# One hybrid decoder layer on eight cores: shared q/k/v weight pieces for two tiles, GLA steps in the next stage, stores from the scrap buffer

## The chip, the cores and the metric

The kernel runs on all 8 cores of one Trainium2 chip. Each core computes the whole layer for one of the 8 batch entries (4096 rows of 1024), and no core talks to another. The metric is the device time in microseconds of the slowest core. The kernel before takes 1694.6 us (median of 3 runs, 1691.15 to 1695.91).

## The reference

For x of one batch entry (4096 x 1024) the layer computes, in short:

```python
h = rms_norm(x, g_pre)
qa, ka, va, za, qb, kb, vb, zb, lr, gate_a, gate_b = split(h @ w_in)   # 5648 columns
# mixer A: 4 heads, two q/k maps of 64 each, causal, ALiBi
p = softmax(q k^T / 8 + bias);  oa = (p[0] - lam * p[1]) @ v
ya = (rms_norm(oa, g_sub_a) * (1 - lam_init) * silu(za)) @ w_up_a
# mixer B: gated linear attention, 4 heads, key 64, value 128
glog = log_sigmoid(lr @ w_alpha + b_alpha) / 16      # lr: 16 columns of the projection
S_t = diag(exp(glog_t)) S_{t-1} + k_t^T v_t ;  ob_t = q_t S_t
yb = (rms_norm(ob, g_sub_b) * silu(zb)) @ w_up_b
y = sigmoid(gate_a) * ya + sigmoid(gate_b) * yb
out = x + rms_norm(y @ w_out, g_post)
```

## The kernel before, in words

The 4096 rows are cut into 8 tiles of 512. After a prologue there is one stage per tile, t = 0 to 7, and a tail. In stage t the attention of tile t (4 heads, 4t+4 blocks of 128 keys each, two blocks per step) is the base load; between its steps TensorE is given "units" of the other work, taken from one list in order. `stage_units(t)` makes the list, each unit has a cost, and `pump` takes units so that their cost keeps pace with the attention steps. The list of stage t is, in order:

- head of E: the first four merge-gate chains of tile t-1 (`GA0`, `GB0`), and `za` of tile t (SiLU gate of mixer A);
- the rest of E(t-1): gates and the two up-projections; then F(t-1): the output projection, the post-norm and the residual (`u_f`), whose `fin(s)` adds x and stores 128 rows;
- gproj(t): low-rank decay (`wlr`, `walpha`), `vb`, `zb`, q/k of mixer B; merged into it, from stage 1 on, `a_units(t+1)`: load x, norm, and transposes of the next tile into `hT`;
- `u_qkv(t+1)`: q, k and v of mixer A for the next tile, with the GLA steps of tile t (`g_khat`, then per 128 rows `g_at`, `g_o`, `g_s`, `g_ew`, `g_tr`, `g_ew2`) merged into it. The last stage has no `u_qkv`, and there the GLA steps follow gproj.

A "chain" is 8 matmuls of 512 columns into one PSUM bank. Five banks rotate among all units and the attention scores. All engines run their instructions in the order of the program text, and a wait at the head of one holds everything behind it.

Weights come in "pieces" (1 MB of float32). The first time, a piece is loaded in four DMAs of 256 KB to a staging area (8 buffers, two pieces), converted to bf16 by VectorE and ScalarE in turn, and written back to DRAM (`wsc`, 512 KB); later it is loaded from there. The converted pieces live in a ring of 7 slots (`wring`), filled in the order of `wseq`: `emit_load` issues the next load, `acquire` takes a piece, `release` frees it. The q/k/v pieces are six: `QA0, QA1, KA0, KA1, VA0, VA1`. All input DMAs stand in SyncE's queue, in order. The stores (`out`, `wsc`) stand in GpSimd's.

x arrives in three buffers `xb0..2` (and four more in the prologue): for the residual of F and for the norm of the next tile. In `fin(s)` VectorE writes the result over the x buffer, GpSimd stores that buffer, and the next x load into it (`x_load(sem)`) waits for the store. The scrap buffer `scr` has six parts, `s0..s5`: F uses s0 to s3 (two per 128 rows, in turn), the E gates too, the decay `gl` (s0, s1), `cum` (s2, s3) and `eb` (s4, s5), and the GLA output o of a step stands in `gl`, that is s0 or s1. The low-rank projection is 8 matmuls that write 16 PSUM partitions each.

`posts` are the pieces of work at the end of each attention head (norm, gate, transpose of the head's output); `run_post` runs one.

## Time and profile before

| | |
|---|---|
| median of 3 runs | 1694.6 us (1691.15 to 1695.91) |
| the profiled execution, its own time | 1694.94 us |
| its span on the slowest core (core 4) | 1693.4 us; the cores lie between 1667.6 and 1693.4 |
| busy: TensorE, VectorE, ScalarE, GpSimd | 1449.6, 874.9, 850.1, 172.0 us |
| DMA, mean | 124 GB/s; 176.09 MB read from and 32.51 MB written to HBM |
| stage ends of 0, 1, 2, ... 7 (about) | 187, 383, 563, 753, 952, 1167, 1394, 1632 us |

TensorE is busy 86% of the span and is what all stages turn on; the other engines are half used. So the page is read by stretches: where TensorE stands still, what it waits for, and at which clock it runs. A "busy" matmul counts from its start to a modelled end, and neighbours overlap, so 100% busy is a full pipeline. "PEclk" is the granted clock as a share of 2.4 GHz; in single stretches it is 1.00 or 0.50.

### The profile page before, as it was taken

The page shows a single profiled execution, that of the slowest core. Times are in us where ns is not written, and L with a number is a line of the kernel's source. Part 1 is how long each engine was busy: PE and PEld are TensorE (multiplying, and loading weights), DVE is VectorE, ACT ScalarE, POOL GpSimd, SP SyncE. Part 2 cuts the span into 40 slices and gives each one's busy share as a digit, 9 for nine tenths or more (in the row PEclk, how much of TensorE's full clock was granted, in tenths as well). Part 3 has the DMA queues.
Part 4 walks back from the last instruction along what each step waited for, and adds up shares of the span by engine and source line. Part 5 has one row for each costly group of instructions (what it writes and reads, how often), then busy time and mean ns, then how long its engine had stood idle before and what let it go on. Part 6 is the DMA issues. An engine that isn't in the chain of part 4 may idle for free.

```text
span 1693.4 us, 28068 instructions; the slowest of 8 cores (1667.6 to 1693.4 us)
## 1 busy us (share of the span) xinstructions
PE 1449.6 (86%) x10512; PEld 756.4 (45%) x10512; DVE 874.9 (52%) x2292; ACT 850.1 (50%) x1714; POOL 172.0 (10%) x247
## 2 busy tenths in 40 slices
PE   3686769779987999889988999888997999998887
PEld 1233324344434454445544554445554555544443
DVE  2467646565546636563446544365335562342564
ACT  2451344514552456435573456735666656667532
POOL 1111101110010001110010000101001010000001
...
GB/s 259 302 214 110 104 278 207 214 51 116 100 200 96 96 104 170 140 52 100 75 201 110 63 100 76 187 87 76 76 63 202 98 63 64 76 75 137 51 75 100
DMA packets 77232, 210.41 MB, mean 124 GB/s; under 512 B 9120, under 2 KB 27824, under 8 KB 77104
## 3 DMA queue, kind: packets, MB, share of 16 engines
...
q0 software_dynamic: 8928, 32.51, 4.8%
...
q10 hardware_dynamic: 1936, 0.94, 0.2%
...
HBM read 176.09 MB, written 32.51 MB: 123 GB/s over the span
## 4 chain that ended last, share of the span: by engine, by line
PE 58%; DVE 20%; ACT 9%; DMA 7%; issue 3%; POOL 2%; SPq 0%; POOLq 0%; DVEq 0%; ACTq 0%
PE ps_q L270 27%; PE ps_f L270 19%; PE ps_oa L270 10%; ACT sb_PT L947 4%; DMA sb_KT<-w_in 3%; DMA sb_xb<-x 2%; DVE sb_gtB L745 2%; DVE sb_state L721 2%; DVE sb_ATs L731 2%; DMA out<-sb_xb 1%; DVE sb_gtA L1002 1%; DVE sb_tmpo L975 1%; DMA sb_KT<-w_up_b 1%; DVE sb_xb L834 1%; ACT sb_wring L378 1%
## 5 line engine op out<-in xcount | busy, mean ns | idle before, releaser
L947 ACT ACTIVATE sb_PT<-ps_q 128x512 bf16<-128x512 f32 (+3 forms) x698 | 371.0, 568 | 333.2 <-PE ps_q L270 183.6
L270 PE MATMUL ps_oa<-sb_V,sb_PT 128*128 128x129 bf16 x4224 | 346.0, 223 | 10.7 <-DVE sb_tmpo L975 3.3
L270 PEld LDWEIGHTS ps_oa<-sb_V,sb_PT 128*128 128x128 bf16 x4224 | 289.6, 99 | 139.1 <-issue 30.0
L947 ACT ACTIVATE sb_PT<-ps_f 128x512 bf16<-128x512 f32 (+3 forms) x454 | 251.9, 567 | 152.4 <-PE ps_q L270 96.5
L270 PE MATMUL ps_q<-sb_hT,sb_wring 128*128 128x512 bf16 x1032 | 263.6, 392 | 20.0 <-ACT sb_wring L378 10.3
L270 PE MATMUL ps_f<-sb_hT,sb_wring 128*128 128x512 bf16 x760 | 196.3, 394 | 6.8 <-ACT sb_hT L596 4.1
L270 PE MATMUL ps_q<-sb_QT,sb_KT 64*128 64x512 bf16 (+3 forms) x698 | 167.9, 369 | 19.9 <-DVE sb_vb L664 4.9
L270 PE MATMUL ps_q<-sb_wring,sb_hT 128*128 128x512 bf16 x528 | 140.2, 405 | 20.4 <-DVE sb_eblast L655 7.4
L270 PEld LDWEIGHTS ps_q<-sb_hT,sb_wring 128*128 128x128 bf16 x1032 | 94.7, 100 | 133.9 <-issue 51.2
L270 PE MATMUL ps_f<-sb_QT,sb_KT 64*128 64x512 bf16 (+3 forms) x454 | 137.5, 368 | 14.1 <-DVE sb_KT L603 4.3
L270 PE MATMUL ps_f<-sb_wring,sb_hT 128*128 128x512 bf16 x496 | 130.1, 396 | 7.5 <-DVE sb_szA L619 3.6
L270 PEld LDWEIGHTS ps_f<-sb_hT,sb_wring 128*128 128x128 bf16 x760 | 69.8, 100 | 90.8 <-issue 32.6
L270 PEld LDWEIGHTS ps_q<-sb_wring,sb_hT 128*128 128x128 bf16 x528 | 49.6, 103 | 84.4 <-issue 46.1
L270 PE MATMUL ps_q<-sb_wring,sb_yT 128*128 128x512 bf16 x320 | 78.1, 379 | 8.8 <-DVE sb_scr L853 4.6
L997 POOL TENSOR_TENSOR sb_rstda<-sb_rsa,sb_lams 128x4 f32<-128x4 f32 x32 | 32.5, 1015 | 454.1 <-DVE sb_rsa L995 451.1
L796 DVE SCALAR_TENSOR_TENSOR sb_scr<-sb_scr,ps_q 128x512 f32<-128x512 f32 x40 | 27.4, 684 | 93.9 <-PE ps_q L270 93.8
L772 ACT ACTIVATE sb_scr<-ps_q 128x512 f32<-128x512 f32 x72 | 43.3, 603 | 63.6 <-PE ps_q L270 63.4
L378 ACT ACTIVATE sb_wring<-sb_KT,sb_smalls 128x256 bf16<-128x256 f32 (+1 forms) x72 | 35.9, 547 | 75.9 <-DVE sb_wring L382 57.7
L270 PEld LDWEIGHTS ps_f<-sb_wring,sb_hT 128*128 128x128 bf16 x496 | 45.2, 101 | 63.3 <-issue 28.7
L772 ACT ACTIVATE sb_scr<-ps_f 128x512 f32<-128x512 f32 x56 | 33.9, 606 | 54.8 <-PE ps_f L270 54.7
L270 PEld LDWEIGHTS ps_q<-sb_QT,sb_KT 64*128 64x128 bf16 x698 | 36.4, 94 | 55.8 <-issue 36.6
L1002 DVE SCALAR_TENSOR_TENSOR sb_gtA<-sb_oaf,sb_rstda,sb_szA 128x128 bf16<-128x128 f32 x128 | 45.7, 357 | 27.8 <-POOL sb_rstda L997 25.0
...
## 6 DMA issues: line engine op xcount, KB each, us to landing
...
```

The costliest lines, as they stand in the source:

```text
L270: P.op("pe", lambda e: e.matmul(out=out_, lhsT=lhsT, rhs=rhs, start=start, stop=stop, **kw), reads=reads, writes=writes)
L378: act(lambda e: e.activation(out=dst_ap, in_=src_ap, func=AF.Copy, scale=sc), rd, [key])
L721: dve(lambda e, c=c, hh=hh, r=r: e.scalar_tensor_tensor(out=state[r, c, :], in0=state[r, c, :], scalar=eblast[r, c, s:s + 1], in1=BANK[b][ ...
L731: dve(lambda e, hd=hd, i=i: e.scalar_tensor_tensor(out=ATs[:, hd, :], in0=o[:, hd * 128:(hd + 1) * 128], scalar=1.0, in1=o[:, hd * 128:(hd ...
L745: dve(lambda e, hd=hd, i=i, sl=sl: e.scalar_tensor_tensor(out=gtB[:, hd, :], in0=o[:, sl], scalar=rstdb[:, i:i + 1], in1=szB[:, s, sl], op ...
L772: act(lambda e: e.activation(out=dst, in_=BANK[b][:, :], func=AF.Tanh, scale=0.5), [b], [key])
L796: dve(lambda e: e.scalar_tensor_tensor(out=ta[j], in0=ta[j], scalar=1.0, in1=BANK[b][:, :], op0=ALU.add, op1=ALU.mult), [b, f"s{j}"], [f"s ...
L834: dve(lambda e, hh=hh: e.scalar_tensor_tensor(out=ap[:, hh * 512:(hh + 1) * 512], in0=zg[hh], scalar=rstdz[:, g:g + 1], in1=ap[:, hh * 512 ...
L947: act(lambda e, pp=pp, m=m, c0=c0, b=b, cbias=cbias: e.activation(out=PT[pp][:, m, c0:512], in_=BANK[b][:, c0:512], func=AF.Exp, bias=cbia ...
L975: dve(lambda e: e.tensor_tensor(out=tmpo[:, i0:i0 + n, :], in0=src[:, :, 0:128], in1=rz[:, i0:i0 + n].unsqueeze(2).to_broadcast([128, n, 1 ...
L997: pool(lambda e: e.tensor_tensor(out=rstda[:, c4], in0=rsa[:, c4], in1=lams[:, 5:6].to_broadcast([128, 4]), op=ALU.pow), [f"rsa{h}", "nhal ...
L1002: dve(lambda e, a=a: e.scalar_tensor_tensor(out=gtA[gi][:, a, :], in0=oaf[:, a, :], scalar=rstda[:, h * 4 + a:h * 4 + a + 1], in1=szA[:, a ...
```

## The change

1. Prologue. Tiles 0 and 1 share the q/k/v pieces: q and k of tile 0, q and k of tile 1, then v of both are computed before stage 0, and `wseq` loses one round of the six pieces (`QKV` for tile 1). Stage 0 has no `u_qkv` any more.
2. GLA steps. `core_units` takes the GLA steps of tile t-1 into the head of stage t, between the half chains of the head gates and of `za`; `merge` now puts side units also into the middle of a chain. In the last stage the steps of tile 7 still follow gproj. The output o of a step stands in `eb` (s4, s5) instead of `gl` (s0, s1).
3. Stores. `fin` writes its result over `scr` and stores from there; the x buffer is free once VectorE has read it.
4. Decay input. `wlr` gets 32 columns per k-chunk (16 of them zero); chunk k goes to one of four groups of 32 PSUM partitions, and `walpha`, repeated four times over the partitions, sums the groups in its own matmul. Both arrive in one array of the host, `w_alr`.
5. Constants move behind the first two weight pieces on SyncE's queue, `gpost` behind the prologue's q and k, and the first x load stands first. `run_post` runs once after each unit with a cost.

```diff
-            def lr_one(b, k, st_, sp_):
-                mm(BANK[b][0:16, :], wlr[:, k, :], hT[t % 2][:, k, :], st_, sp_, ["wlr"] + hkeys(t), [b])
+                g, half = k % 4, k // 4
+                mm(BANK[b][32 * g:32 * g + 32, :], wlr[:, 2 * g + half, :], hT[t % 2][:, 2 * g + half, :], half == 0, half == 1,
+                   ["wlr"] + hkeys(t), [b])
...
-            u_lr = chain(8, lr_one, lr_ev)
+            u_lr = chain(8, lr_one, lr_ev, 0.08)
...
-        wseq = QKV + SEQ_Z + SEQ_G + (QKV if ntiles > 1 else [])
+        wseq = QKV + SEQ_Z + SEQ_G
...
-            dve(lambda e: e.tensor_copy(out=gl[s % 2], in_=BANK[b][:, :]), [b], [f"s{s % 2}"])
+            dve(lambda e: e.tensor_copy(out=eb[s % 2], in_=BANK[b][:, :]), [b], [f"s{4 + s % 2}"])
...
                 for hh in range(2):
-                    dve(lambda e, hh=hh: e.scalar_tensor_tensor(out=ap[:, hh * 512:(hh + 1) * 512], in0=zg[hh],
+                    dve(lambda e, hh=hh: e.scalar_tensor_tensor(out=zg[hh], in0=zg[hh], scalar=rstdz[:, g:g + 1],
...
-                P.op("pool", lambda e: e.dma_start(out=out[g * 128:(g + 1) * 128, :], in_=ap), reads=keys, dma="st" + sem[1:])
+                P.op("pool", lambda e: e.dma_start(out=out[g * 128:(g + 1) * 128, :],
+                                                   in_=scr[:, 2 * (s % 2):2 * (s % 2) + 2, :].rearrange("p a b -> p (a b)")),
+                     reads=[f"s{2 * (s % 2)}", f"s{2 * (s % 2) + 1}"], dma=f"st{s % 2}")
                 x_load(sem)
...
             for i, u in enumerate(main):
                 res.append(u)
-                if u[2]:
-                    continue
...
+        def core_units(k, gap):
+            none = (gap, lambda: None, False)
+            core = [w(0.6 * k, g_khat), none]
+            for s in range(4):
+                core += [w(0.3 * k, g_at, s)]
+                core += [z(g_ew2, s - 1)] if s >= 1 else [none]
+                core += [w(0.6 * k, g_o, s), w(0.3 * k, g_s, s), z(g_ew, s)]
+                if s >= 1:
+                    core += [w(0.4 * k, g_tr, s - 1)]
+            return core + [z(g_ew2, 3)]
...
-                units = head[0:4] + [w(0.4, g_tr, 3)] + head[4:] + before(units, drain_posts) + body + u_f(t - 1)
+                units = merge(head + before(units, drain_posts), core_units(1.0, 0.0) + [z(lambda: None), w(0.4, g_tr, 3)]) + body + u_f(t - 1)
...
-            if nxt:
-                units = units + merge(u_qkv(t + 1), core)
-            else:
-                units = units + core
+            if t + 1 == ntiles:
+                units = units + core_units(3.0, 1.0)
+            elif t >= 1:
+                units = units + u_qkv(t + 1)
...
+        run_units(merge(pro_fm(0, "QA", ev_q), a1[0:5]))
...
+        run_units(merge(pro_fm(0, "KA", ev_k), a1[5:]))
+        emit_load()
+        if two:
+            run_units(pro_fm(1, "QA", ev_q))
+        release(2)
+        if two:
+            run_units(pro_fm(1, "KA", ev_k))
+        release(2)
+        consts("sp", "cstC", [(gpost[:], gpost_d, "gpost")])
+        run_units(tm_chunk([0, 1] if two else [0], QKV[4:6], ev_v))
...
                     c, f, _ = units.pop(0)
                     f()
                     done[0] += c
+                    if c > 0:
+                        run_post()
```

What the change does to the order of the instructions is shown at four places.

TensorE, around the start of tile 1's q (a matmul that reads `sb_hT` and then `sb_wring` makes q or k, the reverse makes v, `sb_QT,sb_KT` are attention scores). Before, q of tile 1 begins in the second half of stage 0, among the last attention steps of tile 0:

```order
L270 MATMUL ps_q<-sb_wring,sb_hT 128x512 x8
L270 MATMUL ps_f<-sb_hT,sb_wring 128x512 x4
L270 MATMUL ps_oa<-sb_V,sb_PT 128x129 x6
L270 MATMUL ps_f<-sb_QT,sb_KT 128x256
L270 MATMUL ps_q<-sb_QT,sb_KT 128x256
L270 MATMUL ps_q<-sb_QT,sb_KT 128x128 x2
L270 MATMUL ps_f<-sb_negm,sb_ident 128x128
L270 MATMUL ps_q<-sb_negm,sb_ident 128x128 x3
L270 MATMUL ps_f<-sb_hT,sb_wring 128x512 x12
```

After, at the same place of the work:

```order
L270 MATMUL ps_f<-sb_hT,sb_wring 128x512 x8
L270 MATMUL ps_q<-sb_hT,sb_wring 128x512 x24
L270 MATMUL ps_f<-sb_hT,sb_wring 128x512 x16
L270 MATMUL ps_q<-sb_hT,sb_wring 128x512 x16
L270 MATMUL ps_q<-sb_wring,sb_hT 128x512 x8
L270 MATMUL ps_f<-sb_wring,sb_hT 128x512 x16
L270 MATMUL ps_q<-sb_wring,sb_hT 128x512 x24
L270 MATMUL ps_f<-sb_wring,sb_hT 128x512 x16
L270 MATMUL ps_q<-sb_wring,sb_hT 128x512 x8
```

All q, k and v of tiles 0 and 1 now stand in one run, ahead of the first score matmul. 96 matmuls have moved from stage 0 to the prologue.

TensorE, the second GLA step (128 rows) of tile 2 (`sb_qtT,sb_ktT` is `g_at`; `sb_vb,sb_ATs` in `g_o` reads what VectorE makes of it). Before, inside q/k/v of tile 3:

```order
L270 MATMUL ps_q<-sb_hT,sb_wring 128x512 x4
L270 MATMUL ps_oa<-sb_V,sb_PT 128x129 x8
L270 MATMUL ps_q<-sb_hT,sb_wring 128x512 x4
L270 MATMUL ps_f<-sb_qtT,sb_ktT 128x256 x2
L270 MATMUL ps_q<-sb_stbf,sb_qtT 128x128
L270 MATMUL ps_q<-sb_vb,sb_ATs 128x128
L270 MATMUL ps_q<-sb_stbf,sb_qtT 128x128
```

After, inside the head gates of the next stage:

```order
L270 MATMUL ps_f<-sb_hT,sb_wring 128x512 x4
L270 MATMUL ps_q<-sb_qtT,sb_ktT 128x256 x2
L270 MATMUL ps_f<-sb_hT,sb_wring 128x512 x4
L270 MATMUL ps_oa<-sb_V,sb_PT 128x129 x8
L270 MATMUL ps_f<-sb_stbf,sb_qtT 128x128
L270 MATMUL ps_f<-sb_vb,sb_ATs 128x128
L270 MATMUL ps_f<-sb_stbf,sb_qtT 128x128
```

`g_o` stood right behind `g_at`; now half a chain and eight matmuls of the attention stand between them.

VectorE, in the tail, the third block of 128 rows of F (L853, now L851, evicts a chain to `scr`; L834, now L831, is `fin`). Before:

```order
L853 TENSOR_TENSOR sb_scr<-ps_q,sb_gpost 128x512 [waits s_act]
L864 TENSOR_TENSOR sb_rsz<-sb_ssz 128x1
L866 TENSOR_SCALAR sb_rsz<-sb_rsz 128x1 [waits s_dve]
L853 TENSOR_TENSOR sb_scr<-ps_q,sb_gpost 128x512 [waits s_act]
L834 SCALAR_TENSOR_TENSOR sb_xb<-sb_scr,sb_rstdz,sb_xb 128x512 [waits s_x0,s_pool]
L834 SCALAR_TENSOR_TENSOR sb_xb<-sb_scr,sb_rstdz,sb_xb 128x512
```

After:

```order
L851 TENSOR_TENSOR sb_scr<-ps_f,sb_gpost 128x512 [waits s_act]
L862 TENSOR_TENSOR sb_rsz<-sb_ssz 128x1
L864 TENSOR_SCALAR sb_rsz<-sb_rsz 128x1 [waits s_dve]
L851 TENSOR_TENSOR sb_scr<-ps_q,sb_gpost 128x512 [waits s_st0,s_act]
L831 SCALAR_TENSOR_TENSOR sb_scr<-sb_scr,sb_rstdz,sb_xb 128x512 [waits s_x0,s_pool]
L831 SCALAR_TENSOR_TENSOR sb_scr<-sb_scr,sb_rstdz,sb_xb 128x512
```

The eviction now waits for the store of the block two before (`s_st0`), because that store reads the same part of `scr`; `fin` no longer writes `xb`.

SyncE's queue, the last part of stage 7 and the tail. Before:

```order
L320 DMA sb_xb<-x 128x1024 [waits s_st1]
L320 DMA sb_xb<-x 128x1024 [waits s_st2]
L320 DMA sb_xb<-x 128x1024 [waits s_st0]
L478 DMA sb_wring<-wsc 128x2048
L478 DMA sb_wring<-wsc 128x2048 [waits s_pe] x3
L320 DMA sb_xb<-x 128x1024 [waits s_st1]
```

After:

```order
L318 DMA sb_xb<-x 128x1024 [waits s_dve] x3
L473 DMA sb_wring<-wsc 128x2048 [waits s_pe] x4
L318 DMA sb_xb<-x 128x1024 [waits s_dve]
L473 DMA sb_wring<-wsc 128x2048 [waits s_pe] x15
L318 DMA sb_xb<-x 128x1024 [waits s_dve]
```

The x loads here waited for stores (`s_st...`); now they wait for VectorE (`s_dve`), which reads the x buffer.

## Rows read from the trace of the kernel before

Times in these views are microseconds, unless marked ns.

**Rows 1.** The page: its head, and busy time of TensorE.
```profile
span 1693.4 us, 28068 instructions; the slowest of 8 cores (1667.6 to 1693.4 us)
PE 1449.6 (86%) x10512; PEld 756.4 (45%) x10512; DVE 874.9 (52%) x2292; ACT 850.1 (50%) x1714; POOL 172.0 (10%) x247
```

**Rows 2.** Windows: length, PE, PEld, DVE, ACT, POOL busy, PE clock, DMA share, GB/s.
```profile
0.00:73.00 73.00, 35.30 (x153) 15.58 (x154) 27.28 (x74) 26.99 (x47) 12.47 (x25) 0.88 0.95 274
73.00:129.00 56.00, 46.40 (x250) 21.09 (x251) 33.57 (x79) 28.33 (x54) 6.41 (x9) 0.88 0.77 238
129.00:187.00 58.00, 42.19 (x253) 21.66 (x252) 44.37 (x148) 11.01 (x27) 9.54 (x12) 0.82 0.27 86
187.00:206.00 19.00, 12.49 (x71) 6.03 (x70) 8.68 (x27) 6.16 (x13) 2.43 (x3) 0.82 0.53 167
206.00:290.00 84.00, 65.66 (x361) 30.17 (x358) 48.24 (x118) 37.29 (x85) 10.34 (x18) 0.94 0.76 232
403.00:468.00 65.00, 62.97 (x423) 31.77 (x421) 34.20 (x78) 30.20 (x67) 3.89 (x6) 1.00 0.33 114
```

**Rows 3.** Waits (total, times, longest): 290 to 870, then the span.
```profile
ACT sb_hb L569 <- DMA sb_xb<-x: 26.2, 6, 6.3
...
PE ps_q L270 <- DVE sb_ATs L701: 26.0, 15, 4.6
PE ps_f L270 <- DVE sb_ATs L701: 11.4, 8, 2.9
```

**Rows 4.** Timeline near 480: SyncE's queue, ScalarE, TensorE; last, TensorE at 1081.
```profile
461.77 13.73 SPq L320 DMA_DIRECT2D sb_xb<-x  x3
...
481.41 1.06 ACT L569 ACTIVATE sb_hb<-sb_xb 128x1024 bf16<-128x1024 f32 x1 [5.12 <-DMA sb_xb<-x]
...
484.14 0.58 PE L270 MATMUL ps_q<-sb_QT,sb_KT 64*128 64x512 bf16 x1 [4.87 <-DVE sb_vb L664]
...
1081.02 1.44 PE L270 MATMUL ps_q<-sb_wring,sb_hT 128*128 128x512 bf16 x3 [3.78 <-DVE sb_eblast L655]
```

**Rows 5.** Windows, q/k/v plus GLA steps, tiles 1 to 6: sum of six.
```profile
sum 275.00, PE 230.07 PEld 127.98 DVE 179.34 ACT 87.23 POOL 32.18; mean PE 38.34 PEld 21.33 DVE 29.89 ACT 14.54 POOL 5.36
```

**Rows 6.** Windows, head gates plus `za`, stages 2 to 7: first, sum of six.
```profile
383.00:402.50 19.50, 18.63 (x123) 9.25 (x121) 10.72 (x40) 10.05 (x19) 2.41 (x3) 1.00 0.35 108
...
sum 150.00, PE 138.24 PEld 72.02 DVE 64.40 ACT 90.46 POOL 12.07; mean PE 23.04 PEld 12.00 DVE 10.73 ACT 15.08 POOL 2.01
```

**Rows 7.** Lines on VectorE, 906 to 951.4: busy, mean ns, idle before.
```profile
L731 DVE SCALAR_TENSOR_TENSOR sb_ATs<-sb_scr 128x128 bf16<-128x128 f32 x16 | 4.9, 304 | 0.5
L745 DVE SCALAR_TENSOR_TENSOR sb_gtB<-sb_scr,sb_rstdb,sb_yT 128x128 bf16<-128x128 f32 x12 | 4.2, 352 | 1.6 <-POOL sb_rstdb L737 1.1
L721 DVE SCALAR_TENSOR_TENSOR sb_state<-sb_state,sb_eblast,ps_q 64x128 f32<-64x128 f32 x12 | 4.1, 344 | 0.4
```

**Rows 8.** The `wlr` matmuls of stage 5, durations and first and last start.
```profile
L270 PE MATMUL ps_q<-sb_hT,sb_wlr x8: 379/379/383, 1064.0 to 1065.5; 128*16 128x512 bf16 x8
```

**Rows 9.** Timeline, PE: two score matmuls that use 64 rows each.
```profile
983.71 0.39 PE L270 MATMUL ps_q<-sb_QT,sb_KT 64*128 64x512 bf16 x1
983.71 0.39 PE L270 MATMUL ps_f<-sb_QT,sb_KT 64*128 64x512 bf16 x1
```

**Rows 10.** Timeline of the end: VectorE and GpSimd; then landings of the stores.
```profile
1678.74 0.69 DVE L853 TENSOR_TENSOR sb_scr<-ps_q,sb_gpost 128x512 f32<-128x512 f32 x1 [0.58 <-ACT sb_junk L851]
1682.19 0.69 DVE L853 TENSOR_TENSOR sb_scr<-ps_f,sb_gpost 128x512 f32<-128x512 f32 x1 [0.58 <-ACT sb_junk L851]
...
1677.59 0.63 POOL L838 DMA_DIRECT2D out<-sb_xb  x1 [2.46 <-DVE sb_xb L834]
1681.05 0.57 POOL L838 DMA_DIRECT2D out<-sb_xb  x1 [2.22 <-DVE sb_xb L834]
...
DMA to landing us min/median/max: 2.9/3.0/5.1
DMA to landing us min/median/max: 2.9/3.4/10.2
```

More of the change, by code:

```diff
@@ L180, in _build @@
         wring = SB("wring", [128, NPIECE, PCOL], BF16)
[L181 to L182 removed]
+        wlr = SB("wlr", [128, 8, 32], BF16)
+        walpha = SB("walpha", [128, 256], BF16)
         xb = [SB(f"xb{i}", [128, 1024], F32) for i in range(3)]
@@ L244, in _build @@
         dma_names = (["stg%d" % i for i in range(8)] + ["wst%d" % i for i in range(NPIECE)] + ["wld%d" % i for i in range(NPIECE)]
-                     + ["cstA", "cstB"] + ["x%d" % i for i in range(7)] + ["st0", "st1", "st2"])
+                     + ["cstA", "cstB", "cstC"] + ["x%d" % i for i in range(7)] + ["st0", "st1"])
         sems = {}
@@ L298, in _build @@
         xseq += [4 * (ntiles - 1) + s for s in range(4)]
-        xst = {"loaded": 0, "used": 0, "limit": 4}
+        xst = {"loaded": 0, "used": 0, "limit": 1}
         XBUF = [(xb[i][:], [f"xb{i}", f"xc{i}"], f"x{i}") for i in range(3)]
@@ L351, in setup_small @@
             dve(lambda e: e.tensor_copy(out=walpha[:], in_=walpha_st), ["ztmp"], ["walpha"])
-            for kc in range(8):
-                dve(lambda e, kc=kc: e.tensor_scalar(out=wlr[:, kc, :], in0=wlr_st[:, kc, :], scalar1=smalls[:, kc:kc + 1],
-                                                     scalar2=None, op0=ALU.mult), ["oafw", "smalls"], ["wlr", "oaf"])
+            dve(lambda e: e.tensor_tensor(out=wlr[:], in0=wlr_st, in1=smalls[:, 0:8].unsqueeze(2).to_broadcast([128, 8, 32]),
+                                          op=ALU.mult), ["ztmp", "smalls"], ["wlr"])
             for hd in range(4):
@@ L912, in stage_units @@
             gproj = u_lr + vbu[0:2] + mid[0:1] + vbu[2:4] + mid[1:3] + vbu[4:6] + mid[3:4] + vbu[6:] + zbu + qku
-            nxt = t + 1 < ntiles
-            if nxt and t >= 1:
+            if t >= 1 and t + 1 < ntiles:
                 gproj = merge(gproj, a_units(t + 1))
             units = units + gproj
-            k = 1.0 if nxt else 4.0
-            core = [w(0.6 * k, g_khat)]
-            for s in range(4):
-                core += [w(0.3 * k, g_at, s), w(0.6 * k, g_o, s), w(0.3 * k, g_s, s), z(g_ew, s)]
-                if s >= 1:
-                    core += [w(0.4 * k, g_tr, s - 1)]
-                core += [z(g_ew2, s)]
-            if nxt:
-                units = units + merge(u_qkv(t + 1), core)
-            else:
-                units = units + core
+            if t + 1 == ntiles:
+                units = units + core_units(3.0, 1.0)
+            elif t >= 1:
+                units = units + u_qkv(t + 1)
             return units
@@ L1030, in _build, with pro_fm @@
         run_units(a_units(0))
-        setup_small()
-        for _ in range(4):
-            emit_load()
-        pro = u_qkv(0)
-        run_units(merge(pro, a_units(1)) if ntiles > 1 else pro)
+        pst = {}
+        def pro_fm(t, nm, ev):
+            res = []
+            for i in range(2):
+                for jj in range(2):
+                    res += fm_chain(t, lambda i=i: pst[f"{nm}{i}"], jj, lambda b, i=i, jj=jj: ev(t, 2 * i + jj, b))
+            return res
+        emit_load()
+        pst["QA0"] = acquire("QA0")
+        emit_load()
+        pst["QA1"] = acquire("QA1")
+        two = ntiles > 1
+        a1 = a_units(1) if two else []
+        run_units(merge(pro_fm(0, "QA", ev_q), a1[0:5]))
+        emit_load()
+        pst["KA0"] = acquire("KA0")
+        emit_load()
+        pst["KA1"] = acquire("KA1")
+        setup_small()
+        run_units(merge(pro_fm(0, "KA", ev_k), a1[5:]))
+        emit_load()
+        if two:
[6 more added lines that the diff above has]
+        run_units(tm_chunk([0, 1] if two else [0], QKV[4:6], ev_v))
         prev = []
@@ L1107 @@
     lamv = np.concatenate([np.asarray(v, f)[0] for v in (lam_q1, lam_k1, lam_q2, lam_k2)])[None, :].repeat(128, 0)
+    w_alr = np.zeros((128, 512), f)
+    for g in range(4):
+        w_alr[32 * g:32 * g + 16, 0:256] = np.asarray(w_alpha, f)[0]
+    w_alr[:, 256:512].reshape(128, 8, 32)[:, :, 0:16] = np.asarray(w_in, f)[0][:, C_LR:C_LR + 16].reshape(8, 128, 16).transpose(1, 0, 2)
     shared = {
```

41 lines of the change are left out of this document (18 added, 23 removed).

## The prediction

> **What bounds the kernel now.** I read the page first. TensorE is busy 1449.6 of the span of 1693.4 us [rows 1], so 244 us are idle; the other engines are about half used, so time is won where TensorE stands still or runs at half clock. Next the windows by stretch. Up to 73 us, where the prologue ends, TensorE is busy 35.3 us and DMA has a share of 0.95 at 274 GB/s: weights and x set the pace. In 129 to 187 (q/k/v of tile 1 with the GLA steps of tile 0) TensorE is busy 42.19 of 58 us at clock 0.82, while DMA is at 0.27. From 206 to 290 (E and F of tile 0, whose 11 remaining weight pieces arrive as float32) E and F take 84 us at a DMA share of 0.76; the same work on converted pieces, 403 to 468, takes 65 us with TensorE busy 62.97 [rows 2]. Later stages have two weak places. In gproj ScalarE waits for x, 26.2 us in six waits [rows 3]. In the windows with GLA steps TensorE is busy 230.07 of 275 us [rows 5], and over the span it waits 26.0 and 11.4 us for the masked scores of `g_at` [rows 3].
>
> **The change part by part.** The sum is made against the profiled execution's 1694.9 us, which is 0.3 us above the median of the runs.
>
> *Prologue, stage 0, and up to the end of F(0).* Tile 1's q, k and v are 12 chains, 96 matmuls. Eight successive `wlr` matmuls of the same 512 columns start within 1.5 us, 0.215 us apart [rows 8], so the 12 chains are 20.6 us at full clock. TensorE idles 37.7 of the first 73 us [rows 2], mostly waiting for pieces; q and k of tile 1 come while `VA0` and `VA1` arrive, the four chains of v after them. I let half hide: the prologue ends at 83. Stage 0 then keeps za and gproj (56 us) and takes the attention steps that stood in the next window, some 8 us: 147. Nothing is left of 129 to 187 but the GLA steps, which go to stage 1. There VectorE carries them: 16 squares (304 ns), 16 gate products (352), 16 state updates (344) [rows 7] are 16.0 us, and with accumulator reads, four masks, four copies, transposes' copies about 26 us. With the 8.7 us that VectorE has in 187 to 206 [rows 2] the head takes 35, say 36 us instead of 19. E and F then start at 183. Their pieces begin to be fetched in stage 0, so I take nearly the clean length, 67 us for 84. End of F(0): 83 + 64 + 36 + 67 = 250 instead of 290, **-40**. Does DMA allow it? The five windows up to 290 moved 61 MB (length by GB/s of each row); without one round of six 0.5 MB pieces it is 58 MB in 250 us, 232 GB/s, under the 274 of the first stretch. Bounds: nothing hides and E stays at 84: 94 + 64 + 36 + 84 = 278, -12. All hides and the head is short: 78 + 60 + 30 + 65 = 233, -57.
>
> *x loads.* Before, SyncE's queue stands at x loads that wait for stores, here for most of 13.73 us; ScalarE has the next tile's square at its head and waits 5.12 us for x, and TensorE then stands 4.87 us [rows 4]. After, x is asked for when VectorE has read the buffer, 3 to 6 us earlier (a store lands 3.4 us after its issue in the median, at most 10.2 [rows 10]). The weights behind it move too. The 26.2 us lie in stages 1 to 4. Not all comes back: in stage 5 TensorE stands 3.78 us at the same place [rows 4] though ScalarE waits for no x there, behind the scans of the decay, and that will then be late next in each stage. I take **-14**; bounds 0 and -26.
>
> *Column groups.* Eight `wlr` matmuls take 1.72 us a tile [rows 8]. If four groups run at once, two turns, 0.43 us: 1.3 saved a tile, 10 in all. If they run one after another: 0. No row has column groups, but two score matmuls on 64 rows each start at the same 983.71 [rows 9], the nearest row. Some of the saving falls into waits: **-6**, bounds 0 and -10. The Trainium skill (TensorEngine Tiling (Array Packing), Key Properties) says that changing the tiling mode drains TensorE, and (TensorE: Matmul & The Clock Gate, Part 3) that three column groups gave 2.38 times the speed. By that speed, as an estimate, the term would be -8, less a drain on either side; no run here shows it yet.
>
> *GLA steps one stage later, tiles 1 to 6.* Six windows of 275 us with 44.9 idle [rows 5] lose about 5 us each of GLA matmuls (30) and most of the idle: -75. The six heads that get them are 150 us with TensorE busy 138.24 and VectorE 64.40 [rows 6]. There VectorE would need 26 more minus what of the steps already trails in (3): 10.7 - 3 + 26 = 34 us. TensorE needs 19 to 31 us plus 5. So the first four heads go to 34, limited by VectorE, the last two to 35 and 37: 208, and 1 each for imperfect overlap, 214: +64. Net **-11**; I write -12 with what earlier head posts bring. `g_o` no longer follows `g_at` directly, which speaks for the gain; the wait moves from latency to VectorE's load, which limits it. Bounds: +10 (VectorE at 85% there) and -35 (its backlog runs into E, which has room).
>
> *F's evictions wait for stores.* The eviction of block s+2 into `scr` waits for the store of block s; VectorE is in order, so the second `fin`, gate products and head posts stand behind it, and behind those TensorE's banks. In the stages two chains and attention lie between, 5 to 7 us, against 3.4 to land: +3 over all, bounds 0 and +20. In the tail there is no attention. The eviction at 1678.74 needs the store issued at 1677.59, landing 3.0 later at 1680.6: 1.9 late. The next store then leaves at about 1683 instead of 1681.05 and lands at 1686 to 1688, while its eviction stood at 1682.19: 4 to 5.5 late, and all behind it moves. The fourth x load comes earlier, but was not last: **+4.5**, bounds +3 and +7 [rows 10].
>
> Constants, `gpost` and the new order of posts: 0; they lie under the first 73 us of loads, or under matmuls, bounds -3 and +2.
>
> Sum: -40 - 14 - 6 - 12 + 3 + 4.5 = -64.5, so 1630.
>
> **The rivals.**
>
> *More is won (1590).* The chain of weights loses its hold altogether, and VectorE's backlog runs into E: -55 - 20 - 9 - 27 + 2 + 4 = -105. For it: E has VectorE busy only 34.20 of 65 us [rows 2]. Against it: `drain_posts` and the deadlines of `g_tr` before the first up-projection.
>
> *Weights hold stage 1 (1673).* E still runs at 84 us because staging has two pieces and the ring seven, and the prologue pays for all 12 chains; heads are limited by VectorE: -12 - 14 - 6 + 3 + 7.5 = -21.5. For it: DMA share 0.76 there. Against it: 0.27 just before, and the round of reloads is gone.
>
> *Slower: stores gate F (1725).* Every store is now on VectorE's path. If under the loads that now start earlier stores land in about the 10.2 us of the longest one [rows 10], the two evictions and the two decay tiles that reuse `scr` in each of seven stages wait about 3.5 us each: 7 x 4 x 3.5 = 98. With the 72 won elsewhere and the tail's 4.5 that is 1694.9 - 72 + 98 + 4.5 = 1725. It decides from a mean landing above some 8 us. Against it: the median of 3.4.
>
> *The column groups do nothing*: 6 us more, 1636, inside the forecast's own range; the clock dips after gaps stay too.
>
> **How the numbers follow.** Forecast (1605 to 1650): 0.54. More won: 0.20. Weights hold: 0.18. Column groups alone not working, near 1636: 0.04. Slower: 0.04. The range of 1588 to 1668 takes in half of each side case. A difference within 0.3% (5 us) can't be told from no change in this kernel. Faster by over 0.3%: 0.94; within: 0.02; slower: 0.04.
>
> **What would show it.** Right: first attention scores near 83 to 88 us, last of stage 0 near 147, F(0) ending near 250; no ScalarE wait for x of over 2 us; DVE near full in the heads of stages 2 to 4, and windows with q/k/v at 32 to 36 us; eight `wlr` starts in two groups of four; in the last 15 us two waits of VectorE for `out`. Wrong: E of stage 1 still over 80 us with DMA above 0.75 (weights), heads over 38 us (VectorE), or waits for `out` in every F (stores).

## The result, and the profile after

The changed kernel takes 1736.95 us (median of 4 runs, 1736.6 to 1738.88); the kernel before, in the same session, took 1695.26 us. The ratio is 1.0252, 95% interval 1.0232 to 1.0272: 2.5% slower, where the forecast was 1630 us, 3.8% faster. Some executions of any kernel on all 8 cores take some per cent longer, with the cores of one die at a lower clock; all times and ratios below leave them out, which leaves b3 only two times and no interval.

Head of the page, and TensorE's row [rows 1]:
```profile
span 1735.4 us, 27926 instructions; the slowest of 8 cores (1719.7 to 1735.4 us)
PE 1434.2 (83%) x10325; PEld 760.4 (44%) x10512; DVE 875.8 (50%) x2285; ACT 853.7 (49%) x1714; POOL 173.2 (10%) x247
```
The engines do the same work. By its row TensorE's idle time grew from 244 to 301 us, but the row has 10325 matmuls where 10512 weight loads were made: 187 records are missing, at the row's mean of 0.139 us some 26 us of work. So idle time grew to about 275 us, an estimate. Where? I cut both spans at the first attention score of stage 2 and of stage 7. The columns of the windows are those of [rows 2]. Before:
```profile
0.00:385.00 385.00, 276.02 (x1540) 131.90 (x1540) 222.02 (x607) 137.51 (x276) 54.90 (x86) 0.88 0.63 192
385.00:1394.90 1009.90, 914.01 (x6970) 486.66 (x6968) 524.50 (x1361) 545.22 (x1100) 94.72 (x131) 0.98 0.33 110
1394.90:1693.40 298.50, 259.59 (x2007) 137.81 (x2006) 128.40 (x326) 167.39 (x338) 22.38 (x31) 0.97 0.25 84
```
After:
```profile
0.00:345.40 345.40, 260.32 (x1453) 125.14 (x1480) 200.41 (x529) 136.66 (x276) 50.12 (x78) 0.89 0.66 206
345.40:1428.40 1083.00, 919.49 (x6835) 495.66 (x6962) 525.66 (x1359) 549.68 (x1100) 94.75 (x130) 0.95 0.31 103
1428.40:1735.40 307.00, 254.35 (x2042) 139.60 (x2074) 149.69 (x398) 167.34 (x338) 28.34 (x39) 0.98 0.25 81
```
At the start of stage 2 the changed kernel is 39.6 us ahead. Stages 2 to 6 then take 73 us longer. TensorE is busy 5 us more by the rows, some 23 us more if the 135 missing records are added at their mean, at a mean clock of 0.95 instead of 0.98. The last stage with the tail takes 8.5 us longer. So the loss lies in the steady stages: some 50 us of idle time, the rest work at half clock. The forecast had looked for a gain there.

The first stretch in its parts: prologue, stage 0, head of stage 1, E and F of tile 0:
```profile
0.00:86.00 86.00, 56.98 (x259) 26.03 (x264) 37.41 (x86) 29.79 (x50) 13.90 (x26) 0.90 0.89 263
86.00:152.00 66.00, 49.27 (x297) 24.12 (x301) 43.00 (x124) 32.32 (x70) 9.11 (x12) 0.87 0.62 193
152.00:197.00 45.00, 28.80 (x177) 14.77 (x177) 36.12 (x123) 14.91 (x31) 9.66 (x13) 0.82 0.36 106
197.00:279.00 82.00, 67.57 (x372) 31.37 (x380) 49.09 (x125) 35.10 (x81) 11.65 (x19) 0.90 0.76 240
```
Next the waits over the span (total, times, longest), and the two transfers of [rows 10] and [rows 3] in the list of DMA issues (count, size, median us to landing):
```profile
DVE sb_scr L851 <- DMA out<-sb_scr: 41.1, 12, 6.2
PE ps_q L1010 <- DVE sb_gtA L1001: 22.5, 11, 5.4
ACT sb_scr L636 <- DMA out<-sb_scr: 19.2, 4, 6.1
PE ps_f L1010 <- DVE sb_gtA L1001: 17.6, 5, 4.4
PE ps_q L270 <- DVE sb_scr L851: 11.6, 7, 3.8
PE ps_f L270 <- DVE sb_scr L851: 7.2, 5, 3.8
ACT sb_hb L564 <- DMA sb_xb<-x: 5.3, 2, 3.2
...
sb_xb<-x SPq DMA_DIRECT2D x60, 512.0 KB, 4.6
out<-sb_scr POOLq DMA_DIRECT2D x32, 512.0 KB, 6.6
```
Before, ScalarE's wait for x over the whole span was:
```profile
ACT sb_hb L569 <- DMA sb_xb<-x: 28.8, 8, 6.3
```
Three things are to be seen. ScalarE's wait for x went from 28.8 to 5.3 us, as forecast. A store now lands 6.6 us after its issue, not 3.4, and VectorE and ScalarE wait 60 us for such landings. And TensorE waits 40 us in front of the transposes of `gtA` (line 1010), the last piece of an attention head. One of these, at the start of the up-projection of stage 4, in the timeline:
```profile
806.66 1.01 POOL L996 TENSOR_TENSOR sb_rstda<-sb_rsa,sb_lams 128x4 f32<-128x4 f32 x1 [22.48 <-DVE sb_rsa L994]
807.70 1.51 DVE L1001 SCALAR_TENSOR_TENSOR sb_gtA<-sb_oaf,sb_rstda,sb_szA 128x128 bf16<-128x128 f32 x4 [1.12 <-POOL sb_rstda L996]
809.36 0.58 PE L1010 MATMUL ps_f<-sb_ident,sb_gtA 128*128 128x128 bf16 x4 [4.39 <-DVE sb_gtA L1001]
```
A gap of this kind (5.4, 4.4, 4.4, 4.4, 3.9 us) stands once in each of stages 2 to 6, at 403, 600, 809, 1028 and 1255 us.

The windows that answer to [rows 6] and [rows 5], heads with GLA steps (first, sum of six) and q, k, v without (sum of six):
```profile
345.00:382.00 37.00, 27.59 (x193) 15.03 (x196) 29.57 (x102) 13.04 (x24) 7.10 (x9) 0.91 0.21 70
...
sum 244.00, PE 194.34 PEld 114.00 DVE 184.33 ACT 124.88 POOL 42.37; mean PE 32.39 PEld 19.00 DVE 30.72 ACT 20.81 POOL 7.06
...
sum 296.00, PE 261.14 PEld 139.52 DVE 130.31 ACT 115.38 POOL 7.05; mean PE 43.52 PEld 23.25 DVE 21.72 ACT 19.23 POOL 1.18
```
The heads grew by 94 us (64 forecast), to 37 to 46.5 us each with VectorE busy 68 to 82%. The q, k, v windows here also hold the chains of mixer B's q and k in front, which [rows 5] left out; the same stretches took 379 us before, so they lost 83 (75 forecast). The windows together are 11 us longer, where the forecast had them 11 us shorter.

The tail, [rows 10]'s answer:
```profile
1713.67 0.63 POOL L834 DMA_DIRECT2D out<-sb_scr  x1 [2.46 <-DVE sb_scr L831]
1718.86 0.69 DVE L851 TENSOR_TENSOR sb_scr<-ps_q,sb_gpost 128x512 f32<-128x512 f32 x1 [4.63 <-DMA out<-sb_scr]
1724.20 0.69 DVE L851 TENSOR_TENSOR sb_scr<-ps_q,sb_gpost 128x512 f32<-128x512 f32 x1 [2.47 <-DMA out<-sb_scr]
```
Two evictions wait 4.63 and 2.47 us for stores, where the forecast had 1.9 and 4 to 5.5. From the first eviction of this last F to the end of the span it is 27.5 us (1707.90 to 1735.4), before 21.6 (1671.83 to 1693.4): 5.9 us more, where the forecast had 4.5 with bounds of 3 and 7.

### The profile page after: what moved, and what is told of

Same layout as the page of the kernel before. It is cut to its first block, busy times and chain, and to the rows that moved or that the text cites. A ratio compares the mean times of both kernels' runs of the same rounds, so it can differ in the third digit from the quotient of the medians.

```text
span 1735.4 us, 27926 instructions; the slowest of 8 cores (1719.7 to 1735.4 us)
## 1 busy us (share of the span) xinstructions
PE 1434.2 (83%) x10325; PEld 760.4 (44%) x10512; DVE 875.8 (50%) x2285; ACT 853.7 (49%) x1714; POOL 173.2 (10%) x247
## 4 chain that ended last, share of the span: by engine, by line
PE 52%; DVE 22%; ACT 10%; DMA 9%; issue 4%; POOL 2%; SPq 1%; POOLq 0%; DVEq 0%; ACTq 0%
PE ps_q L270 24%; PE ps_f L270 17%; PE ps_oa L270 9%; DMA out<-sb_scr 6%; ACT sb_PT L946 4%; DMA sb_KT<-w_in 2%; DVE sb_state L718 2%; DVE sb_scr L831 2%; DVE sb_gtA L989 2%; DVE sb_gtA L1001 2%; DVE sb_ATs L728 1%; ACT sb_ztmp L613 1%; DVE sb_qtT L671 1%; DVE sb_gtB L742 1%; DVE sb_tmpo L974 1%
## 5 line engine op out<-in xcount | busy, mean ns | idle before, releaser
L946 ACT ACTIVATE sb_PT<-ps_q 128x512 bf16<-128x512 f32 (+3 forms) x690 | 361.8, 564 | 245.4 <-PE ps_q L270 148.7
L270 PEld LDWEIGHTS ps_oa<-sb_V,sb_PT 128*128 128x128 bf16 x4224 | 293.7, 100 | 135.1 <-issue 29.9
L270 PE MATMUL ps_f<-sb_hT,sb_wring 128*128 128x512 bf16 x677 | 177.8, 395 | 16.5 <-ACT sb_hT L591 6.0
L270 PE MATMUL ps_q<-sb_wring,sb_hT 128*128 128x512 bf16 x568 | 154.0, 403 | 18.0 <-DVE sb_szA L614 3.8
L270 PE MATMUL ps_f<-sb_wring,sb_hT 128*128 128x512 bf16 x401 | 110.0, 407 | 14.7 <-DVE sb_eblast L652 4.0
L270 PEld LDWEIGHTS ps_f<-sb_hT,sb_wring 128*128 128x128 bf16 x712 | 66.3, 101 | 92.1 <-issue 37.3
L270 PEld LDWEIGHTS ps_q<-sb_wring,sb_hT 128*128 128x128 bf16 x600 | 56.3, 102 | 82.8 <-issue 42.2
L270 PE MATMUL ps_q<-sb_wring,sb_yT 128*128 128x512 bf16 x282 | 71.7, 387 | 16.9 <-DVE sb_scr L851 10.9
L270 PE MATMUL ps_f<-sb_wring,sb_yT 128*128 128x512 bf16 x209 | 56.4, 405 | 12.3 <-DVE sb_scr L851 7.2
L270 PEld LDWEIGHTS ps_f<-sb_wring,sb_hT 128*128 128x128 bf16 x424 | 40.2, 103 | 57.6 <-issue 29.2
```

What stands on the lines that cost most here:

```text
L270: P.op("pe", lambda e: e.matmul(out=out_, lhsT=lhsT, rhs=rhs, start=start, stop=stop, **kw), reads=reads, writes=writes)
L946: act(lambda e, pp=pp, m=m, c0=c0, b=b, cbias=cbias: e.activation(out=PT[pp][:, m, c0:512], in_=BANK[b][:, c0:512], func=AF.Exp, bias=cbia ...
```

## The experiments

All ratios are to the kernel before, run beside it on the same chip.

| kernel | ratio | 95% interval |
|---|---|---|
| changed | 1.0252 | 1.0232 to 1.0272 |
| a1: deferred pieces at their old places | 1.0303 | 1.0269 to 1.0337 |
| a2: stores from the x buffer | 1.0142 | 1.0116 to 1.0168 |
| a3: GLA steps at the old place | 1.0152 | 1.0126 to 1.0178 |
| a4: decay input on 16 partitions | 1.0242 | 1.0221 to 1.0263 |
| a5: a1, a2, a3 together | 1.0086 | 1.0055 to 1.0117 |
| a6: a2, a3 together | 0.9986 | 0.9953 to 1.0019 |
| a7: a6, but tile 0's steps in stage 1 | 0.9939 | 0.9914 to 0.9963 |
| b1: before, stores from scrap | 1.0217 | 1.0191 to 1.0242 |
| c1: changed, list not emptied | 1.0125 | 1.0090 to 1.0160 |
| c2: c1 and a2 | 1.0030 | 1.0009 to 1.0052 |
| b2: b1 with three pairs of buffers | 1.0133 | 1.0074 to 1.0193 |
| a8: a7, list not emptied | 0.9939 | 0.9915 to 0.9963 |
| b3: b1, x refill waits for the store | (1694.14 and 1699.41 us) | |
| c3: c1, x refill waits for the store | 1.0031 | 1.0005 to 1.0057 |
| a9: a7 and a4 | 0.9830 | 0.9773 to 0.9887 |
| a10: a7, cost 0.26 | 0.9816 | 0.9730 to 0.9901 |
| a11: a9, list not emptied | 0.9803 | 0.9738 to 0.9868 |
| c4: c2 and a4 | 0.9922 | 0.9888 to 0.9956 |

### One part undone at a time

**a1**, `run_post()` back at its two old places and out of the unit loop.

> The changed kernel with one part undone: run_post is called at the old places of a step (five times per pair of key blocks) and not once after each unit. TensorE waits 40.1 us for the head's gate product (gtA, L1001) in the changed kernel and 19.9 us before, about 4.4 us of it once in each E. Theory P (posts now reach TensorE before VectorE is ready): about 20 us less than the changed kernel, 1717 us, and the 4.4 us gaps in E go. Theory S (stores from scr hold VectorE) and theory H (heads limited by VectorE): within 3 us of the changed kernel, 1737.

1747.05 us; by the ratios 0.5% slower than the changed kernel: the pieces after every unit are a help. Not the cause.

**a2**, the final sum back into the x buffer, stored from there.

> The changed kernel with the stores and fin as before (result over the x buffer, stored from there; the next x load waits for the store). Theory S: VectorE waited 41.1 us for stores and the stores take 6.6 us to land instead of 3.4; with the old stores 25 to 35 us less than the changed kernel, 1705 us, and no wait of VectorE for out. Theories P and H: at most 5 us either way (the tail gives 4.5 back, the x loads take up to 14 in stages 1 to 4), 1732 to 1745.

1721.77 us: 1.1% back, half of what its theory asked for.

**a3**, the steps back beside q, k, v, or bare in stage 0.

> The changed kernel with the GLA steps at their old place (merged into q/k/v of the next tile, in stage 0 behind gproj) and the old merge. Theory H (the head of a stage is limited by VectorE, and its backlog delays E): heads back from 244 to about 150 us in sum, q/k/v windows back up by 83, E bodies 7 us shorter each; stage 0 longer by 10: 35 to 45 us less than the changed kernel, 1695 us. Theories S and P: the windows cancel (+94 against -83), so 10 us less at most, 1727 to 1740.

1721.95 us: 1.0% back, under half of what its theory asked for. Stages 2 and 3 took 179.1 and 189.8 us, as before (180.0, 189.1), but stage 2 started 30 us later than in the changed kernel: what tile 0's steps saved in stage 0 was given up.

**a4**, decay input on 16 partitions, its chain's cost back at the default 0.26 a matmul.

> The changed kernel with the decay input as before: 8 matmuls that write 16 PSUM partitions each. All theories: the column groups are no cause. If they ran at once this is 6 to 10 us slower than the changed kernel (1745); if their gain falls into waits, within 3 us; if the mode switch costs more than it gives, 3 us faster.

1737.87 us, no difference. This held only here, as a9 shows below.

### Parts together, and the stores alone

**a5** and **a6** are the changed kernel with two or three parts undone; **a7** splits the steps by tile:
```
 if t == 1:  head merged with core_units(1.0, 0.0)   # tile 0's steps
 else:       head as before
 end of stage t >= 1:  merge(u_qkv(t + 1), core)     # tile t's steps, as before
```

> The changed kernel with three of its parts undone together: GLA steps back beside the q, k, v of the next tile, stores back from the x buffer, deferred attention pieces back at their old places. What is left of the change is the shared q/k prologue, the decay input in column groups and the order of the constants. Theory 'two costs that add' (GLA steps in the heads cost some 12 us of TensorE idle time in each of stages 2 to 6, the stores some 33 us over stages 4 to 7 and the tail, as the stage lengths of the kernel with old GLA steps show): stage 2 starts near 375 and stages 2 to 7 take what they took before (1308 us), so about 1687, 10 us faster than before. Rival 'the prologue only shifts work' (what it wins up to stage 2 comes back later because VectorE or the weight stream is late): 1697 or more. Rival 'the deferred pieces matter by themselves': stages 2 to 7 longer or shorter than before by over 5 us.

> The kernel of the run before in this call, but with the deferred attention pieces after every unit with a cost, as in the changed kernel. In the changed kernel, putting them back cost 13 us. Theory 'the pieces after every unit help wherever the GLA steps stand': 1672 to 1680. Rival 'they helped only since the heads were crowded': same as the run before, 1684 to 1690.

> The kernel of the run before in this call, but tile 0's GLA steps stand in the head of stage 1 (as in the changed kernel) and not bare in stage 0; tiles 1 to 7 have theirs at the old place, beside q, k, v or in the last stage. Stores from the x buffer. Theory 'two costs that add': stage 0 ends near 152 in place of 180, stage 1 takes some 20 us more than the changed kernel's 193 for the second set of steps, stage 2 starts near 364, and stages 2 to 7 take 1308 us: about 1675, 20 us faster than before. Rival 'stage 1 is bound by VectorE with two sets of steps in it': stage 2 starts at 375 or later, no better than the run before.

Measured were 1700.95, 1689.7 and 1678.8 us: a5 and a6 missed the times that their theories gave, a7 came near. a5, which is before with the shared prologue, the column groups at their cost of 0.08 and the constants' order, is 0.9% slower than before; how much of that is the cost number (see a10) no run separates. a6 with the pieces after every unit is 1.0% better and equals before. a7 beats before by 0.6%: stage 2 starts at 353.5 instead of 385 us, but stages 2 to 7 take 1323.6 us instead of 1308.4.

**b1** puts a single part into the kernel before:
```
-  out=ap[:, hh * 512:(hh + 1) * 512] ... out[g] <- ap
+  out=zg[hh]                         ... out[g] <- scr pair s % 2; x_load(sem)
```

> The kernel before with one part of the change alone: the final sum is written into the scrap buffer, stored from there, and the x buffer is refilled without waiting for a store. Theory 'two costs that add': the store costs the changed kernel 15 us (what it gained when it was undone) to 33 us (what stages 2 to 7 lose with it when only the GLA steps are put back), so 1712 to 1730. Rival 'the stores cost only through the slots of the weight stream that the later x loads shift in the changed kernel': 1697 to 1702. The forecast's own term was +3 in the stages and +4.5 in the tail against -14 for earlier x loads: 1690.

1723.8 us, **2.2% slower by this one edit**. The forecast had -14 + 7.5 for it. Its waits and stores:
```profile
DVE sb_scr L854 <- DMA out<-sb_scr: 35.3, 13, 5.1
ACT sb_scr L639 <- DMA out<-sb_scr: 16.5, 3, 10.4
PE ps_q L270 <- DVE sb_scr L854: 15.3, 9, 3.9
...
out<-sb_scr POOLq DMA_DIRECT2D x32, 512.0 KB, 6.3
```

### Is it the wait, or what runs beside the store?

**b2**, `s % 2` becomes `s % 3` for the scrap pairs, so only the fourth block of a tile reuses a stored pair.

> The kernel before with the final sum stored from the scrap buffer (2.2% slower than the kernel before), but with three pairs of scrap buffers in turn in place of two, so that only the fourth block of a tile waits for a landing, that of the store three blocks earlier. Theory W 'the cost is VectorE's wait for the landing of the store of two blocks earlier, and TensorE's wait behind it': 1694 to 1704. Rival X 'the cost is that the x loads are issued earlier and stand before or beside stores and weight pieces': 1718 to 1735.

1713.22 us: between the two forecasts, so inconclusive. VectorE's wait is gone (1.9 us in the span), but the fourth block is now stored from the first pair (s0, s1), which the decay's activation writes next, and the wait moved there (42.2 us in seven waits); in its timeline:
```profile
864.47 0.58 POOL L837 DMA_DIRECT2D out<-sb_scr  x1 [1.75 <-DVE sb_scr L834]
873.65 0.69 ACT L639 ACTIVATE sb_scr<-ps_f,sb_nbal 128x512 f32<-128x512 f32 x1 [7.89 <-DMA out<-sb_scr]
874.48 3.55 PE L270 MATMUL ps_f<-sb_wring,sb_hT 128*128 128x512 bf16 x8 [6.03 <-ACT sb_scr L639]
```
**b3** keeps b1's order of instructions on every engine and adds one wait (in short):
```
+ x_load:  writes=keys + ["h" + sem]
+ store:   reads=[..., "h" + sem]       # the refill waits for the landing
```

> The kernel before with the final sum stored from the two pairs of scrap buffers (2.2% slower), but each x refill waits for the landing of the store of the same block, as in the kernel before; the order of instructions on every engine is the same. Theory X 'the store lands in 6.3 us in place of 3.4 because the x refill (and weight pieces) run beside it, and VectorE and ScalarE wait for that landing': the store's median comes back to about 3.4 us, the waits for it nearly go, and the time is 1695 to 1705. Rival W 'any wait of VectorE for a store of two blocks earlier costs this much': 1715 to 1728.

Its two times, 1694.14 and 1699.41 us, stand against a median of 1692.1 of before. The store lands in 3.2 us again in the median. The same store and the same eviction in stage 4, b1 first:
```profile
856.51 17.36 SPq L320 DMA_DIRECT2D sb_xb<-x  x3
856.78 0.63 POOL L837 DMA_DIRECT2D out<-sb_scr  x1 [4.21 <-DVE sb_rz L974]
863.36 0.69 DVE L854 TENSOR_TENSOR sb_scr<-ps_q,sb_gpost 128x512 f32<-128x512 f32 x1 [3.94 <-DMA out<-sb_scr]
864.20 0.58 PE L270 MATMUL ps_q<-sb_QT,sb_KT 64*128 64x512 bf16 x1 [3.90 <-DVE sb_scr L854]
```
b3:
```profile
840.71 0.63 POOL L837 DMA_DIRECT2D out<-sb_scr  x1 [4.21 <-DVE sb_rz L974]
844.96 13.20 SPq L320 DMA_DIRECT2D sb_xb<-x  x3
845.03 0.69 DVE L854 TENSOR_TENSOR sb_scr<-ps_q,sb_gpost 128x512 f32<-128x512 f32 x1 [1.68 <-DMA out<-sb_scr]
845.87 0.37 PE L270 MATMUL ps_q<-sb_QT,sb_KT 64*128 64x512 bf16 x1 [1.64 <-DVE sb_scr L854]
```
In b1 the refill leaves SyncE 0.27 us before the store leaves GpSimd, and the store needs 6.6 us; with the refill held back it needs some 4.3, and TensorE's gap falls from 3.90 to 1.64 us. The added wait holds back all loads that stand behind the refill in SyncE's queue too; in b1 the only loads that SyncE issues from 850 to 870 are refills. **c3** makes the same edit in c1:

> The changed kernel without the emptied list in the up-projection (1.25% slower than before), and each x refill waits for the landing of the store of the same block. Theory X: most of the 17 us between it and the same kernel with stores from the x buffer (0.3% slower than before): 1697 to 1703. Rival W: 1708 to 1716.

1697.46 us, from 1.0125 to 1.0031, and equal to c2, which stores from the x buffer. So the wait for a store costs next to nothing if the store lands in 3 us, and the early refill is what made it dear.

### The emptied list

**c1** and **c2**; the edit, in the up-projection (line 804):
```
- (drain_posts(), st.update(u=acquire(f"U{p_}")))
+ (drain_posts() if t == ntiles - 1 else None, st.update(...))
```

> The changed kernel with one thing taken out of it that the kernel before has too: the up-projection of stages 1 to 7 no longer empties the list of deferred attention pieces before it starts (only the tail does). Theory D 'the GLA steps in the heads move the start of the up-projection onto the end of an attention head, so that the emptied list puts the transposes of gtA in front of TensorE while VectorE still works on gtA': the gap of 4.4 us at the start of each up-projection goes, with the half clock behind it, some 6 us in each of stages 2 to 6: 1700 to 1712. Rival H 'the heads themselves are VectorE's': 1730 to 1740.

> The run before in this call, and the stores from the x buffer as in the kernel before (alone that gave 1721.8). Theory D: 1685 to 1697, so that the GLA steps in the heads cost little when both are gone. Rival H: 1715 to 1725.

1713.34 us and 1695.5 us. Against the changed kernel and a2 that is 1.3% and 1.1% back, about what theory D said. In c1's waits TensorE's for `gtA` fell from 40.1 us to
```profile
PE ps_f L1010 <- DVE sb_gtA L1001: 8.4, 5, 3.0
PE ps_q L1010 <- DVE sb_gtA L1001: 6.8, 5, 3.9
```
and in the same place of stage 4 the transposes come at 808.46 with up-projection matmuls of `gaT` at 803.00 and 806.27 ahead of them. The profile has the gain mostly in stages 4 to 6, some 8 us each; stage 2 is 3.4 us shorter and stage 3 not at all, though each had its gap.

> The kernel that was fastest so far (tile 0's GLA steps in stage 1, the others' at the old place, stores from the x buffer, 0.6% faster than before), and the up-projection no longer empties the list. Theory D says that the old place has no long gap there, so little is to be had: 1670 to 1680. If every up-projection waits somewhat for an emptied list: 1660 to 1670.

1681.09 us, ratio as a7's: at the old place the emptied list costs nothing.

### The decay input's order

> The fastest kernel so far (tile 0's GLA steps in stage 1, the others' at the old place, stores from the x buffer, 0.6% faster than before) with the decay input on 16 partitions as before in place of column groups. In the changed kernel that made no difference; here the gap of 2.6 us in front of the decay input's copy stands in each stage. If it is the groups' (they end later, since the copy waits for all eight): 1670 to 1676. If not: 1678 to 1683; if the groups save what they seem to, some 0.3 us for each of 8 stages, no difference can be seen either.

> The kernel of the run before in the list of fastest ones (1.7% faster than before, decay input on 16 partitions), but with the column groups back and the planner's cost of the decay input left at 0.26 a matmul, so that the order on TensorE is the same in both. With groups and the changed kernel's cost of 0.08 it was 0.6% faster than before. Theory N 'what cost 17 us was the number 0.08: it took the attention work away from between the two halves of the decay input and behind it, so that TensorE waited for the copy and the decay': 1660 to 1665, and the groups themselves save no more than 0.4 us a stage. Rival G 'the groups cost, since their matmuls or the copy of 128 partitions are slow': 1675 to 1683.

a9 gave 1662.25 us, 1.1% better than a7 and faster than either of its forecasts, and a10, which has the groups but the old cost number, 1661.8. So the groups are innocent, and the number 0.08 is the cost. In a7's stage 4 all eight `wlr` matmuls stand together, and one attention step behind them is too little to cover VectorE's queue:
```profile
824.49 0.61 PE L270 MATMUL ps_q<-sb_hT,sb_wlr 128*32 128x512 bf16 x8
828.29 0.68 DVE L628 CAST sb_gtB<-ps_q 128x512 bf16<-128x512 f32 x1
829.12 2.66 PE L270 MATMUL ps_q<-sb_wring,sb_hT 128*128 128x512 bf16 x8 [2.58 <-DVE sb_gtB L628]
```
In a10 attention stands between the halves, and no gap of this kind follows:
```profile
826.03 0.40 PE L270 MATMUL ps_q<-sb_hT,sb_wlr 128*32 128x512 bf16 x4
826.36 0.63 PE L270 MATMUL ps_oa<-sb_V,sb_PT 128*128 128x129 bf16 x8
827.45 0.40 PE L270 MATMUL ps_q<-sb_hT,sb_wlr 128*32 128x512 bf16 x4
828.57 0.68 DVE L628 CAST sb_gtB<-ps_q 128x512 bf16<-128x512 f32 x1
```
Over the span TensorE waits for this copy 7.4 us in a7, in stages 4, 6 and 7 and not in each stage as the expectation of a9 had it, and 0.6 us in a10. Of the 15 us between the two profiles 8.9 lie in stage 4 and 4.1 in the last. So the gap shown is a part of the price; the rest lies in what else the number moves in the plan, and was not taken apart. Why a4 did not show it in the changed kernel stays open; there stages 2, 4 and 6 were some 3 us shorter each, and stage 1 and the last stage 3 and 2 us longer.

### What is left of the new place

> The changed kernel with its GLA steps in the heads, but with all three costs found so far taken out: stores from the x buffer, no emptied list in the up-projection, decay input on 16 partitions at 0.26 a matmul. Without the last it was 0.3% slower than before. If the rest of the difference to the kernel with GLA steps at the old place is the decay input's order: 1680 or less. Rival H2 'the heads themselves lack work beside VectorE (their own gaps of 1.6, 1.2 and 2.7 us in stage 4)': 1685 to 1697, some 20 to 30 us behind the fastest.

> The fastest kernel so far (1.7% faster than before), and the up-projection no longer empties the list of deferred pieces. Without the 17 us of the decay input's order a small gain might show that did not show before: 1655 to 1662 if every up-projection waits a little for the list, 1660 to 1665 if not.

c4 gave 1679.37 us (0.9922), a11 1659.45 us (0.9803). They differ only in where the steps of tiles 1 to 6 (and the last tile's weights in the plan) stand: 1.2%. c4's own time just meets the first forecast (1680 or less), but it lies 20 us behind the fastest, as H2 had it, so it does not tell the two apart. By the ratios the heads keep a cost of their own of 1.2%, with intervals of 0.3 and 0.7%. a11 is the fastest kernel and beats both; a9, a10 and a11 can't be told apart. Its windows, cut as above:
```profile
0.00:352.10 352.10, 267.32 (x1540) 129.56 (x1540) 219.53 (x600) 137.47 (x276) 55.45 (x86) 0.92 0.66 203
352.10:1360.20 1008.10, 914.67 (x6970) 487.57 (x6968) 524.65 (x1361) 546.06 (x1100) 94.77 (x131) 0.98 0.32 110
1360.20:1658.40 298.20, 260.41 (x2007) 138.45 (x2006) 128.43 (x326) 167.47 (x338) 22.37 (x31) 0.97 0.25 83
```
It is 33 us ahead at stage 2, and then takes before's 1308 us to within 2.

## Why the prediction was wrong

Steps on a chain from the changed kernel to a11: list 1.27% (c1), refill beside the store 0.94% (c3, which equals c2), decay input's order 1.08% (c2 to c4), steps of tiles 1 to 6 in the heads 1.19% (c4 to a11). Together 4.5% of 1695, 76 us. The ends of a step come from different chips in part, so each has an error of 0.3 to 0.7%. The chain was followed in this order only. The sizes depend on it: b1's edit costs 2.2% in the kernel before, the new place 1.6% (a6 to a2), and both together less than their sum.

- *Prologue, stage 0, up to the end of F(0), -40.* The places were right (first score at 86, stage 0 ending at 152, no reload round), the size was not: F(0) ended at 279, not 250, so -11. The head took 45 us instead of 36, and E and F 82 instead of 67, at the DMA share of 0.76 they had before. This is the rival "weights hold stage 1", which the text had priced and should have given more weight: that one stretch has the same eleven pieces to fetch in either kernel. The 39.6 us at stage 2 came true only because tile 1's steps had not been paid yet. a7's 353.5 and a11's 352.1 are the honest number: -32.
- *x loads, -14.* The step that failed worst. The wait went away (28.8 to 5.3 us over the span) and the time did not come: the same early issue put the refill beside the store, whose landing doubled. c1 to c3 shows it cost 16 us, though in c3 ScalarE waits 21.3 us for x again; in b1 and b3 it is the whole of the edit's price. What the shorter wait would be worth alone no run shows. The prediction had both halves, an x load "3 to 6 us earlier" and a store on VectorE's path, and did not join them: the store's 3.4 us was read from a kernel in which the refill of its buffer waits for it.
- *F's evictions wait for stores, +3 in the stages and +4.5 in the tail.* Mechanism right: waits in every F, as "wrong (stores)" had announced. In the stages the size hung on 3.4 us. The rival "stores gate F" had the cause (loads that start earlier) and a price of 98 us for landings of 10.2; they were 6.6. The tail's term was right, 5.9 us measured, but its parts were not: the first eviction waited 4.63 us instead of 1.9 (the x load was issued 0.27 us before that store too), and the second 2.47 instead of 4 to 5.5.
- *Column groups, -6.* TensorE's time fell as worked out, eight matmuls from 2 x 1.03 us (a9's rows of the same place) to 2 x 0.40, 1.3 us a tile. That is a ratio of 2.6. The Trainium skill (TensorE: Matmul & The Clock Gate, Part 3) has 2.38 for three groups; the trace agrees in kind. But a9 and a10 take the same time within their intervals of 0.6 to 0.9%, so no gain is shown. The cost number that the diff changed beside them cost 1.1% on a7. The prediction did not weigh that number at all.
- *GLA steps one stage later, -12.* Priced from window to window (+64, -75), measured +94 and -83, so the heads' term was 30 us too small and the sum of the windows has the wrong sign. More lies outside the windows, for the planner's later units all moved. Longer heads put the start of the up-projection onto the end of an attention head, where `drain_posts` lets TensorE meet unfinished work of VectorE: 1.3%. The rest, c4 to a11, is the place itself. The text took a head to be as long as VectorE's work in it, 34 us, and 1 us more for imperfect overlap. VectorE did 30 to 32 us of work there and the heads took 37 to 46.5: it was not full, and TensorE stood in single gaps of up to 2.7 us in stages 2 to 5 (up to 1.0 in 6 and 7) between steps that wait on each other. That these waits are the 1.2% is argued from the rows, not shown by a run.
- *Order of posts, 0.* a1 and a5 against a6 put it at 0.5 to 1.0% in favour of the change. By that, a quarter to a half of a11's 2.0% is this edit.

The rivals on the slower side had 4 in 100 between them. The costs were each bounded at a few us a stage and added as if independent, while six stages repeat every one of them.
